# Two out-projection pieces moved into a recurrence, and the attention's normalising moved between two engines, in a three-block language-model kernel on one core

## The reference, cut to what matters

```python
for l in range(DEPTH):                      # DEPTH = 2
    x = x + 0.5 * _swiglu(...)
    proj = _rms_norm(x, norm_mix[l]) @ w_in[l]
    y_rwkv = _rwkv7_mixer(...)              # state = state*w + sa*b + v*k, step by step
    y_attn = _attention_mixer(...)          # exp(s - lse) @ v, over a band of keys
    y_conv = _conv_mixer(...)               # conv, layer norm, silu
    mix = concatenate([y_rwkv, y_attn, y_conv])
    x = x + mix @ w_out[l]
    x = x + 0.5 * _swiglu(...)
```

## Time and profile before

| what | us |
| --- | --- |
| median of three runs | 1378.06 (1377.97 to 1378.10) |
| the profiled execution, device time | 1380.12 |
| its span, first to last instruction | 1378.3 |
| first mixer: chain begins (first L1530) | 286.50 |
| first mixer: chain ends (first L1557) | 315.94 |
| second mixer: chain begins (first L1530) | 822.42 |

### The profile page before, as it was taken

One profiled execution on the slowest core, in us unless ns is written; L12 is line 12 of the kernel. 1 busy time (PEld: TensorE's weight loads), 2 busy tenths in 40 slices (PEclk: granted clock), 3 DMA queues, 4 the chain that ended last, 5 costly groups with the idle time before them and its releaser, 6 DMA issues.

```text
span 1378.3 us, 24757 instructions
## 1 busy us (share of the span) xinstructions
PE 1348.3 (98%) x9701; PEld 1168.5 (85%) x9701; DVE 980.0 (71%) x1310; ACT 741.7 (54%) x1048; POOL 156.2 (11%) x156
## 2 busy tenths in 40 slices
PE   9999999989999999999999998999999999999997
PEld 7888889977888888888888987788888997788885
DVE  6666666777776666766656766876666665998787
ACT  6444457465744445644447656564444445755553
POOL 3000000097000000000000048300000033000000
PEclk9999999999999999999999999999999999999999
DMA  9756355123475645755529121465553953456630
GB/s 339 265 184 197 112 178 174 34 92 114 150 251 189 197 130 184 261 189 183 183 67 298 55 93 34 127 225 197 187 187 106 305 183 106 152 187 216 197 133 31
DMA packets 170483, 230.57 MB, mean 167 GB/s; under 512 B 4687, under 2 KB 151815, under 8 KB 170149
## 3 DMA queue, kind: packets, MB, share of 16 engines
q1 hardware_dynamic: 167920, 223.75, 49.6%
q10 hardware_dynamic: 1877, 5.59, 1.1%
q0 software_dynamic: 608, 0.12, 0.1%
HBM read 228.39 MB, written 2.63 MB: 168 GB/s over the span
## 4 chain that ended last, share of the span: by engine, by line
PE 89%; DVE 5%; ACT 3%; issue 1%; POOL 1%; ACTq 0%; POOLq 0%; DVEq 0%
PE banks L490 37%; PE banks L658 27%; PE banks L662 14%; PE banks L1530 2%; DVE down_lo L475 1%; DVE gate_lo L475 1%; PE banks L613 1%; PE banks L941 1%; PE banks L1180 1%; PE banks L1393 1%; PE banks L1333 1%; PE banks L1190 1%; DVE up_lo L475 1%; PE banks L1464 0%; PE banks L1202 0%
## 5 line engine op out<-in xcount | busy, mean ns | idle before, releaser
L658 PE MATMUL banks<-hT,up_hi 128*128 128x512 f32 x880 | 220.8, 393 | 0.0
L475 DVE TENSOR_TENSOR down_lo<-w_down,down_hi 128x2048 fp32r<-128x2048 f32 (+1 forms) x65 | 147.8, 2273 | 93.2 <-ACT down_hi L470 93.2
L737 ACT ACTIVATE work<-banks 128x256 f32<-128x256 f32 x176 | 66.8, 384 | 258.6 <-PE banks L662 258.2
L658 PE MATMUL banks<-hT,gate_hi 128*128 128x512 f32 x800 | 199.8, 392 | 0.0
L470 ACT ACTIVATE down_hi<-w_down 128x2048 fp32r<-128x2048 f32 (+1 forms) x65 | 123.6, 1902 | 115.9 <-PE banks L490 115.9
L658 PEld LDWEIGHTS banks<-hT,up_hi 128*128 128x128 f32 x880 | 158.2, 189 | 29.2 <-issue 0.6
L475 DVE TENSOR_TENSOR up_lo<-w_up,up_hi 128x2048 fp32r<-128x2048 f32 x72 | 164.5, 2285 | 15.9 <-ACT up_hi L470 15.9
L475 DVE TENSOR_TENSOR gate_lo<-w_gate,gate_hi 128x2048 fp32r<-128x2048 f32 x64 | 146.9, 2296 | 36.7 <-ACT gate_hi L470 36.6
L658 PEld LDWEIGHTS banks<-hT,gate_hi 128*128 128x128 f32 x800 | 147.0, 188 | 28.4
L490 PE MATMUL banks<-down_hi,ff_hi 128*128 128x512 f32 x400 | 156.2, 391 | 0.0
L490 PE MATMUL banks<-down_lo,ff_hi 128*128 128x512 f32 x400 | 156.2, 391 | 0.0
(11 more groups left out here) (388 smaller groups left out, 2217.4 us busy)
## 6 DMA issues: line engine op xcount, KB each, us to landing
w_up<-in_ffn_w_up_dram SPq DMA_DIRECT2D x44, 1024.0 KB, 5.4
w_down<-in_ffn_w_down_dram SPq DMA_DIRECT2D x44, 1024.0 KB, 5.2
w_gate<-in_ffn_w_gate_dram SPq DMA_DIRECT2D x43, 1024.0 KB, 5.4
w_up<-in_w_in_dram SPq DMA_DIRECT2D x12, 1024.0 KB, 9.5
w_gate<-in_w_up_dram SPq DMA_DIRECT2D x11, 1024.0 KB, 5.0
w_up<-in_w_up_dram SPq DMA_DIRECT2D x11, 1024.0 KB, 5.1
w_down<-in_w_down_dram SPq DMA_DIRECT2D x11, 1024.0 KB, 5.0
w_down<-in_w_in_dram SPq DMA_DIRECT2D x9, 1024.0 KB, 8.4
```

The costliest lines, as they stand in the source:

```text
L475: dve.tensor_tensor(staged[kind][1][:, 0:cols], slot[sl][:, 0:cols], staged[kind][0][:, 0:cols].bitcast(F32), ALU.subtract).then_inc(split ...
L658: pe.matmul(bank[:, :], w[0][:, c, at], hpair[:, :, c, :], start=c == 0, stop=False)
L737: act.activation(to[:, q, j * SEQ:(j + 1) * SEQ], psum[2 * q + j][:, SEQ:], ACT.Copy)\
```

## The change

It has four parts, in both mixers alike.

1. In the chain's first step the product `E2T` of each batch is a "move" where it was a "copy": VectorE empties its banks, ScalarE did.
2. The scaling of the attention's rows goes from VectorE to ScalarE: `normalise` there is two activations with a scale from memory, at i = 0, 1, 4, 6, 10 and 12. VectorE keeps the reciprocal, as `invert`, before the chain and at i = 0, 4, 6, 10 and 12.
3. The pieces (1,1,0,0) and (1,1,0,1) go from the tail into the recurrence, behind the values of ch = 2 and behind the first product of ch = 3.
4. In the tail, PE takes the convolution's variance behind the two pieces (1,0,0,h), not ahead of them, and VectorE takes the low parts 3 and 4 (L2093) ahead of the convolution's mean (L2089).

Ten semaphores are merged into seven with larger counts (`kk_sum`, `qk_sum` and `gn_var` are all `head_sum`, and so on); the waits are for the same events. Cut to the core:

```diff
-        [("copy", "E2", "DT", "D"), ("copy", "E2T", "D", "DT")],
+        [("copy", "E2", "DT", "D"), ("move", "E2T", "D", "DT")],
...
+            def invert(self, h):
+                self.dve.wait_ge(S["exp_done"], 2 * h + 2 + past["exp_done"])
+                self.dve.reciprocal(arec[:, h, :], asum[:, h, :]).then_inc(S["sum_inverted"], 1)
...
+            def normalise(self, h):                                  # ActAttention
+                self.act.wait_ge(S["sum_inverted"], h + 1 + past["sum_inverted"])
+                for t, (lo, hi) in enumerate(((0, P), (P, 3 * P))):
+                    row = self.logit[:, h % 2, lo:hi]
+                    ins = self.act.activation(row, row, ACT.Copy, scale=arec[:, h, t:t + 1])
+                ins.then_inc(S["p_ready"], 1)
...
@@ act_mix, in the loop over the groups
                 if i in (12, 13):
                     prior_values(i - 12)
+                if i in (0, 1, 4, 6, 10, 12):
+                    attention.normalise((0, 1, 4, 6, 10, 12).index(i))
                 if i in (0, 3, 5, 9, 11):
                     attention.exps((0, 3, 5, 9, 11).index(i) + 1)
...
@@ dve_mix
-            attention.normalise(0)
-            attention.normalise(1)
+            attention.invert(0)
...
-                if i in (4, 6, 10, 12):
-                    attention.normalise((4, 6, 10, 12).index(i) + 2)
+                if i in (0, 4, 6, 10, 12):
+                    attention.invert((0, 4, 6, 10, 12).index(i) + 1)
...
@@ pe_mix
                     values_of(1)
+                    out_ready(1, 2)
+                    out_unit(1, 1, 0, 0)
                 if ch == 3:
                     y_of(2).then_inc(S["y_mm"], 1)
+                    out_unit(1, 1, 0, 1)
...
-            out_ready(1, 2)
-            for t, h in HALVES:
-                out_unit(1, 1, t, h)
+            for h in range(2):
+                out_unit(1, 1, 1, h)
+            out_ready(1, 4)
+            for h in range(2):
+                out_unit(1, 0, 0, h)
             pe.wait_ge(S["cl_sq"], 1 + past["cl_sq"])
...
-            out_ready(1, 4)
-            for h in range(2):
-                out_unit(1, 0, 0, h)
             out_ready(2, 4)
```

101 lines of the change are left out of this document (51 added, 50 removed).

## The result

| | median us | runs |
| --- | --- | --- |
| before | 1378.01 | 1377.9 to 1378.1, 4 runs |
| changed | 1390.24 | 1388.92 to 1393.45, 4 runs |

The ratio is 1.0083, with a 95% interval of 1.0060 to 1.0106: slower, by twice what was forecast, and above the range. The second thing to see is the spread: 0.2 us before, 4.5 us after. The profiled execution of the changed kernel is the fastest of its runs, 1388.92 us, so it shows the smallest loss.

What follows compares the result with a forecast made beforehand. The prediction took TensorE, busy for 98% of the span, as the bound. Its terms +1.9 + 1.6 - 0.45 gave +3.05 us per mixer, +6.1 in two, on 1378.06: 1384.2 us, range 1378.0 to 1388.7.

Steps and rivals of the forecast that it cites:

- steps A to D: Chain, from its middle on: scalings on ScalarE delay its split and group 14's product; +1.9 us per mixer (+1.3 to +2.3).
- Step A: Chain's middle: ScalarE's scaling at i = 6 stands ahead of an attention result's copy; +0.7 us, taken in by later delays.
- Part 1: Chain's first step: VectorE empties E2T's banks beside other work; 0, between -0.3 and +0.2 us per mixer.
- Part 3: Recurrence: TensorE is busy without a gap, so two pieces add their whole duration; +1.6 us per mixer.
- Part 4: Tail, up to slot 2: without two pieces TensorE waits 1.1 us for VectorE's split; -0.45 us per mixer (0 to -0.8).
- What comes last is VectorE: Tail: VectorE's sequence, 5.4 to 6.0 us in all and taken as 5.7, sets when slot 2 begins.
- stays hidden: Behind slot 2: VectorE's split of the next slots had over 1 us in hand, so it costs nothing.
- the clock's two rivals: Behind the recurrence, no fall: 1379.6 to 1382 us, chance 0.24; at the chain's end, a second fall: 1387 to 1389.6, 0.20.
- the rival: Behind the recurrence: the full-width second new piece keeps the clock up; 1381.9 us in one mixer, 1379.6 in both; chance 0.24.
- the second: Chain's end: more TensorE waiting lets the clock fall into the recurrence; 2.7 us lost per mixer, at most 3.4; chance 0.20.
- VectorE was the bound at the chain's end: Chain's end: TensorE's waits for VectorE go; -2.0 us per mixer instead of +1.9, 1376.4 us in all; chance 0.10.

Runs made afterwards that it cites:

- d1_changed: The changed kernel as it is, run again on another chip, the same as the filled kernel's second run: median 1395.47 us.
- c2_changed: The changed kernel as it is, run once more on a further chip: median 1394.37 us.
- b1_fill: The changed kernel with four more unread 128x384 products per mixer, two behind group 12 and two behind group 13: 1387.27 us.
- b4_lasttwo: The changed kernel with the scaling of heads 4 and 5 on VectorE again: 1383.99 us, ratio 1.0046.
- d2_filled: The changed kernel with four more unread products per mixer behind groups 12 and 13, beside the changed kernel on one chip: median 1385.81 us, fastest 1385.16.
- b3_bestfill: The kernel before with third and fourth part, convolution's square on ScalarE, and four unread products per mixer in the chain's waits for VectorE: 1378.35 us.
- a1_pieces: The kernel before with the third part alone, two pieces moved from tail to recurrence: ratio 1.0004, runs from 1376.24 to 1383.55 us.
- b2_best: The kernel before with the third and fourth part and the convolution's square on ScalarE, chain unchanged: 1376.71 us, ratio 0.9992.

## Why the prediction was wrong

**The chain (steps A to D): right.** Forecast +1.9 us, measured +1.7 at full clock (31.10 for 29.43 in the second mixer; without a fall the unchanged chain took 28.3 to 29.5 us in other profiles). Step A's 0.7 is there as well, 0.69 us of waiting; in the changed kernel most of it is taken in by the later delays, as the step said. The pair of scalings takes 0.80 us on ScalarE for 0.79 reckoned (VectorE's pairs took from 0.59 to 1.22 us in the profile of before, so the 1.08 of the rows was a long one); TensorE's wait for ScalarE's emptying ahead of group 14's product is 1.03 us there, and one of 0.99 us stands ahead of group 13's; group 14's product runs 1.8 us later in the chain for 2.2 forecast.

**Part 1: right in its place, wrong as a statement on the move.** "0, between -0.3 and +0.2" (measured 0.1) holds only because the second part clears VectorE's queue ahead of it. I priced the instruction and not what stands ahead of it on its new engine.

**Part 3: the working was right against the wrong alternative.** The pieces were to add 1.6 us. They do, to TensorE's work. But at full clock 0.87 us of it fill a wait for VectorE that the profile of before does not have, since the clock was at half there; against a recurrence at full clock they cost 0.4 (24.1 for 23.8 us). So the term was mis-sized by 1.2 us. (The recurrence held five pieces before, not four.)

**Part 4: wrong, and this is a step of the sum that failed.** Forecast -0.45, measured +0.82 in the first mixer. The step was "What comes last is VectorE". I followed TensorE's work and VectorE's, but not the square: GpSimd's square stands behind the mean and TensorE's variance behind the square, and the change moved the mean behind the low parts, where the square falls beside the split. The VectorE sum itself was good: its items add up to 5.34 us (5.7 with a low part at 0.93, so "5.4 to 6.0" was a little high), and with the square on ScalarE the tail took 5.38. The rows held the hint that the square and VectorE delay each other, and I had used it for the low parts alone ("each took 0.93 while GpSimd ran beside it"). The same step said that what lies behind slot 2 "stays hidden": in the second mixer it cost another 1.5 to 1.7 us.

**The sum at full clock.** This is an estimate from the lengths: chain 2 x 1.7, recurrence 2 x 0.4, tail 2 x 0.9 against the 6.0 to 6.15 of before, behind slot 2 1.5: 7.5 us on the 1376.2 us of a run without falls, 1383.7. The filled kernel, whose two chains are 1.2 us longer by the fillers, has its fastest run at 1385.2. The forecast's 1384.2 lay near that by luck: part 3 was too dear and part 4 too cheap, and it stood on a time of before that had falls in it. The merged semaphores (seventeen into seven, not ten) show no price: between the mixers it takes 474.9 us for 474.8.

**The clock: the step that decided the result.** The forecast took the granted clock as unchanged, with the clock's two rivals as alternatives at 0.24 and 0.20. Both came about, one in each place. The fall behind the recurrence went, which gives 1.8 us per mixer against the profile of before; the rival gave the second new piece as the reason, and kernels without the piece lost that fall too. And a longer one came at the chain's end, which takes 5.1 us in the profiled execution (1.5 in the first mixer's chain and 3.6 in its recurrence) and 5.9 in d1_changed. I had priced the second at 2.7 us, as long as the old stretch; it lasted 6.8 to 13.7. And I treated the fall as an on-or-off property of the kernel, from two mixers that agreed in one profile. The runs on other chips, from 1376.1 to 1383.2 for the kernel before, show it as something that varies from one execution to the next. The three profiles of the changed kernel are 5.2, 10.9 and 14.7 us above 1383.7, and the stages in which the clock fell are longer than at full clock by 5.4, 10.6 and 14.7 us; in the last, d1_changed, 5.0 of it lie outside the mixers. That makes the 1389 to 1398 us. Also, of the twelve mixers with the tail's new wait of 2.1 us six had a fall of 3.4 us beginning within 1.5 us of slot 2 (both of c2_changed, the second of d1_changed, b1_fill, b4_lasttwo and of the profiled execution), which the sum did not have either.

**Rivals.** That VectorE was the bound at the chain's end: excluded, as its own condition said; ScalarE's split began 1.3 us later in the chain, not at its old place.

## What to carry to other kernels

Moving an operation to an idle engine is priced by what it is put in front of, there and behind its result, not by its duration or by the engine's busy share; and an order that moves one producer has to be followed through every engine that reads it, GpSimd too. Where TensorE's work is thin, a microsecond of waiting may cost five through the clock, and a wait may be cheaper filled with useless products than left empty (d2_filled), or dearer where falls are rare (b3_bestfill). Where a profile has stretches at the lower clock, read its waits again as they would be at the full one. Take several profiles before you call a fall a property of the kernel, and before you credit a change with its absence: look whether kernels without the change have lost it too.

## What was not expected of the hardware

- A fall of the clock at the same place in the same kernel comes and goes between executions and between two mixers of one execution (a1_pieces: none in the first mixer, 13.7 us at the level of 1.2 GHz in the second). The kernel before ran between 1376.1 and 1383.2 us on four other chips, the slower runs at a lower mean clock, and within 0.2 us on the first. Eight of the seventeen profiles also have a fall of 3.4 us between the mixers, at 749 to 762 us, outside the stages that were changed; it costs about 1.5 us.
- GpSimd's product of 128x512 took 1.28 us beside VectorE's two low parts, which lost 0.6 us, and 3.02 beside VectorE's split of 2.28 us, which lost nothing.
- TensorE stands idle for 0.4 to 0.6 us now and then with nothing to wait for, at places that differ from kernel to kernel. Before, in the first chain; with b2_best, at the start of the first recurrence, which took 25.1 us with it instead of 24.1 (and 25.3 in b4_lasttwo, with 0.93 us at the same place):

```profile
297.03 1.09 PE L1530 MATMUL banks<-work 64*64 64x64 f32 x30 [0.47 <-issue]
```
```profile
316.91 0.74 PE L1557 MATMUL banks<-work,w_gate 64*64 64x64 f32 x19 [0.64 <-issue]
```

  What causes these was not looked into, and they blur lengths by about as much.
